# Dealing the last nine projection pieces anew over the attention heads of a hybrid encoder step

## The reference

```python
proj = h @ w_in                    # fq, fk, fv | rq, rk, rv, rg (3072 columns and 8 forget logits)
o_fox = softmax(q k^T / 8 + cq - ck, causal) @ v       # 8 heads of 64
y_ret = retention(rq, rk, rv)                           # 4 heads of 128
o_ret = silu(rg) * ret_head_norm(y_ret, gn_gain)
x = x + concat(o_fox, o_ret) @ w_out
```

## Time and profile before

| | us |
|---|---|
| median of three runs | 1013.97 |
| lowest, highest | 1012.26, 1021.46 |
| the profiled execution | 1019.17 |
| its span | 1017.4 |
| PE busy | 886.0 |
| DVE busy | 326.9 |
| ACT busy | 209.2 |
| mean granted clock of PE | 0.944 |

### The profile page before, as it was taken

The page is one execution under the profiler, slowest core; times in us unless marked ns, Lnnn a source line. Parts: engine busy times, 40 slices in busy tenths (PEclk is TensorE's granted clock), DMA queues, the critical chain, the costliest instruction groups (busy, mean ns, idle before and its releaser), DMA issues.

```text
span 1017.4 us, 14050 instructions
## 1 busy us (share of the span) xinstructions
PE 886.0 (87%) x5438; PEld 523.0 (51%) x5438; DVE 326.9 (32%) x794; ACT 209.2 (21%) x448; POOL 81.5 (8%) x93
## 2 busy tenths in 40 slices
PE   7999989899989878789768999869999978788873
PEld 5888878688733323323335555437963323233222
DVE  1514433442621101111024688872252101011103
ACT  3413223422211101011123222332121111010110
POOL 1101000000011101011010000000001111111100
PEclk9999989599899999999988999978989999999997
DMA  9713623106969999999978222304247999999965
GB/s 349 305 44 131 164 77 129 42 1 242 424 273 416 418 419 418 420 419 418 408 315 337 84 84 84 100 10 186 104 156 268 420 419 420 419 420 418 419 281 199
DMA packets 47714, 271.12 MB, mean 266 GB/s; under 512 B 10693, under 2 KB 10845, under 8 KB 18904
## 3 DMA queue, kind: packets, MB, share of 16 engines
q1 hardware_dynamic: 34416, 239.66, 58.2%
q0 software_dynamic: 11600, 24.27, 6.9%
q10 hardware_dynamic: 1632, 6.29, 1.6%
HBM read 266.54 MB, written 25.37 MB: 287 GB/s over the span
## 4 chain that ended last, share of the span: by engine, by line
PE 50%; DMA 28%; DVE 5%; issue 2%; ACT 1%; SPq 1%; ACTq 0%; POOLq 0%; DVEq 0%
DMA slot<-in_experts 23%; PE PS L985 10%; PE PS L1076 8%; PE PS L1008 7%; PE PS L826 6%; PE PS L573 3%; PE PS L803 2%; DMA XGT<-rows,IDX 2%; PE PS L966 2%; PE PS L1093 2%; DMA slot<-outs 2%; PE PS L927 1%; SPq L375 1%; PE PS L879 1%; DVE YC L1854 1%
## 5 line engine op out<-in xcount | busy, mean ns | idle before, releaser
L985 PE MATMUL PS<-slot,XG 128*64 128x512 f32 x1024 | 243.7, 621 | 64.6 <-DMA slot<-in_experts 62.5
L985 PEld LDWEIGHTS PS<-slot,XG 128*64 128x64 f32 x1024 | 78.5, 142 | 205.7 <-issue 192.9
L573 PE MATMUL PS<-slot,HT 128*128 128x256 f32 x576 | 135.0, 392 | 7.4 <-ACT HT L1157 7.4
L1738 DVE SCALAR_TENSOR_TENSOR hid_by_token<-PS,SC,SG 128x256 f32<-128x256 f32 x32 | 15.5, 484 | 391.5 <-ACT SG L1314 391.5
L573 PEld LDWEIGHTS PS<-slot,HT 128*128 128x128 f32 x576 | 111.0, 196 | 24.9 <-ACT HT L1157 7.6
L1008 PE MATMUL PS<-slot,HID 128*64 128x512 f32 x512 | 118.0, 603 | 0.9 <-ACT HID L1319 0.9
L1076 PE MATMUL PS<-HC,slot 128*128 128x384 f32 x256 | 86.0, 491 | 1.5 <-DVE HC L1814 1.5
L1314 ACT ACTIVATE SG<-PS,SC 128x256 f32<-128x256 f32 x32 | 15.2, 474 | 268.1 <-PE PS L985 268.1
L1076 PEld LDWEIGHTS PS<-HC,slot 128*128 128x128 f32 x256 | 47.6, 190 | 40.0 <-issue 9.5
L1328 ACT ACTIVATE Y<-PS,SC 128x1024 f32<-128x1024 f32 x32 | 35.6, 1114 | 152.4 <-PE PS L1008 152.4
L1008 PEld LDWEIGHTS PS<-slot,HID 128*64 128x64 f32 x512 | 35.0, 139 | 58.6 <-issue 57.2
(11 more groups left out here) (291 smaller groups left out, 821.0 us busy)
## 6 DMA issues: line engine op xcount, KB each, us to landing
slot<-in_experts SPq DMA_DIRECT2D x192, 1024.0 KB, 21.3
slot<-in_w_pw SPq DMA_DIRECT2D x12, 1024.0 KB, 8.3
slot<-in_w_in SPq DMA_DIRECT2D x11, 1024.0 KB, 10.8
slot<-outs ACTq DMA_DIRECT2D x6, 1024.0 KB, 7.0
slot<-in_w_out SPq DMA_DIRECT2D x4, 1024.0 KB, 5.2
rows<-X POOLq DMA_DIRECT2D x6, 512.0 KB, 8.5
KTC<-in_k_past POOLq DMA_DIRECT2D x1, 2048.0 KB, 13.4
slot<-in_v_past SPq DMA_DIRECT2D x2, 1024.0 KB, 8.3
```

Source lines behind the costliest of these rows:

```text
L573: last = mm(PS[:, in_bank(n), 0:UCOL], HT[:, k, P * t:P * (t + 1)], w[:, k, :], start=k == 0, stop=k == KD - 1)
L985: last = mm(PS[CAP * e:CAP * (e + 1), 2 + p % 2, :], XG[:, p % 2, k, CAP * e:CAP * (e + 1)], w[:, 2 * FE * (k % 4):2 * FE * (k % 4 + 1)], ...
```

## The change

The last nine pieces run in another order, given by a table `PIECES`: after (8,1) come (9,0), (9,1), then the two gate units (10 and 11, all tiles), and last (8,2) and (9,2), the sample tiles' values. PE and ACT place them anew: one between the K heads' transposes and the first scores, one in step 0 ahead of the transposes of the probabilities, none at the end of step 0, then one in steps 1 and 2, two in step 3, one in each of steps 4, 5 and 6. The silu of the gate moves from step 5 to step 4. The factor GN is multiplied into the retention rows after the first tile of the Q heads, long before the loop; in the loop one multiplication is left, in step 6. The retention transposes move to step 7 (tile 0) and step 8 (tiles 1 and 2); the retention projection stays from step 9 on. The waits follow: slots are free by `LAST_PIECE`, so the loads of all four `w_out` units wait for pieces 35 and 36; the sample values' store and the one behind it wait for piece 36.

```diff
+PIECES = [(pos, t) for pos in range(8) for t in range(NT)] + [(8, 0), (8, 1), (9, 0), (9, 1)] + [
+    (pos, t) for pos in (10, 11) for t in range(NT)] + [(8, 2), (9, 2)]
+LAST_PIECE = [PIECES.index((pos, 2)) + 1 for pos in range(N_IN)]
+LATE = (0, 1, 1, 2, 1, 1, 1)
...
-                    sp.wait_ge(S("proj_done"), NT * (i - LO + 1))
+                    sp.wait_ge(S("proj_done"), LAST_PIECE[i - LO])
...
-            pool.wait_ge(S("pj_ready"), 30)
+            pool.wait_ge(S("pj_ready"), 28)
             store(o["fox_v_prompt"][0].rearrange(tiles, p=P), PJ[:, 0:2, VO:RQO], "mix_stored")
+            pool.wait_ge(S("pj_ready"), 36)
             store(o["fox_v_sample"][0].rearrange(flat), PJ[:, 2, VO:RQO], "mix_stored")
...
-                    pe.wait_ge(S("pj_ready"), (26, 29, 30, 30)[i // 4])
+                    pe.wait_ge(S("pj_ready"), (26, 28, 35, 36)[i // 4])
...
+            dense_in(1)
             pe.wait_ge(S("kt_act"), NT)
...
+                if i == 0:
+                    dense_in(1)
                 if i < ITEMS:
                     probs_transposed(i)
                 if i >= 1:
                     weighted_values(i - 1)
-                if i < 6:
-                    dense_in(2 if i < 3 else 1)
+                if i < len(LATE):
+                    dense_in(LATE[i])
+                elif i == 7:
+                    ret_mixed_transposes(0)
                 elif i == 8:
-                    ret_mixed_transposes(0)
                     ret_mixed_transposes(1)
+                    ret_mixed_transposes(2)
                 elif i == 9:
-                    ret_mixed_transposes(2)
                     ret_projected(0)
...
-                    if n == 30:
+                    if n == 28:
                         act.wait_ge(S("k_ready"), NT)
...
+            evacuate(1)
+
             def exps(i):
...
-                if i < 6:
-                    evacuate(2 if i < 3 else 1)
-                if i == 5:
+                if i == 0:
+                    evacuate(1)
+                if i < len(LATE):
+                    evacuate(LATE[i])
+                if i == 4:
                     q.settle()
                     q.do(A(PJ[:, :, RGO:MIX], PJ[:, :, RGO:MIX], ACT.Silu), S("rg_silu"))
                     preload(ACT.Exp)
-                if i in (8, 9):
-                    for t in (range(2) if i == 8 else (2,)):
+                if i in (7, 8):
+                    for t in ((0,) if i == 7 else (1, 2)):
...
+                if t == 0:
+                    dve.wait_ge(S("gn_in"), 16)
+                    tt(PJ[:, :, RQO:RVO], PJ[:, :, RQO:RVO], bc(GN[:, :], 1, NT), ALU.mult)
...
                 if i == 6:
                     dve.wait_ge(S("rg_silu"), 1)
-                    dve.wait_ge(S("gn_in"), 16)
-                    tt(PJ[:, :, RGO:MIX], PJ[:, :, RGO:MIX], bc(GN[:, :], 1, NT), ALU.mult)
-                elif i == 7:
                     tt(PJ[:, :, RGO:MIX], PJ[:, :, RGO:MIX], PJ[:, :, RQO:RVO], ALU.mult, S("mixr_ready"))
```

More of the change, by code:

```diff
@@ L552, in full @@
                 pe.wait_ge(S(f"full{i % LO}"), 16 * (before + i // LO + 1 - first))
-            pieces = iter(range(NT * N_IN))
+            pieces = iter(enumerate(PIECES))
             def in_bank(n):
@@ L560, in dense_in @@
             def dense_in(m):
-                for n in itertools.islice(pieces, m):
-                    pos, t = divmod(n, NT)
+                for n, (pos, t) in itertools.islice(pieces, m):
                     w = dense(pos)
```

## The result

The changed kernel takes 1002.53 us in the median of five runs (1000.49 to 1006.78), the kernel before 1013.97 (1012.26 to 1021.46): a ratio of 0.9874 with a 95% interval of 0.9838 to 0.9911. That is faster by 1.3% (the interval leaves 0.9 to 1.6%), by 11.4 us between the medians and by 13.2 us between the means of the five runs each (1003.10 and 1016.33). The forecast was 996, in a range of 990 to 1004. The profiled execution took 1006.78 us and is the slowest of the five.

What follows compares the result with a forecast made beforehand. PE sets the pace through attention, losing time to waits and a fallen clock. Moving the first retention projection's end from 204.13 to 186.25 saves 17.9 us: 1013.97 - 17.9 = 996.1, forecast 996, range 990 to 1004.

Steps and rivals of the forecast that it cites:

- Start of the loop: Attention loop's start: pieces replace PE waits of 0.90 and 1.96 us; item 0's transposes end at 139.9.
- Steps 1 to 6: Attention loop: five steps of 5.11 us and one of 8.62, together 34.2, so step 6 ends at 174.1.
- Silu: Steps 5 and 6: 5.76 us of PE work against 5.9 us of ACT's block, leaving 0.1 to 0.5 us wait.
- The 2.66 us of the Trainium skill: ACT's table switches: by the page two would be 2.7 us longer, a sum of 998.8 instead of 996.1.
- Steps 7 to 9: Up to the retention projection: 6.9 to 7.0 us of small work plus 1.5 of waits; projection starts at 182.6.
- Loads: Four `w_out` loads leave at about 169.0 and 174.1, hidden by 3 us or more; cost 0.
- The low clock rival: Steps 7 to 9: the clock falls all the same, price 5.8 us, a time of 1002; chance 0.22.
- what the prediction drew from the Trainium skill: Steps 7 to 9: a transpose does not count as busy PE; by that rule the low clock rival is the outcome.
- the sum's base, 204.13: End of the first retention projection in the kernel before, 197.67 + 6.46, from which the forecast 186.25 was subtracted.
- the 17.9 us: Gain at the first retention projection's end: waits gone 8.45, half clock gone 10.9, less new waits 1.5.
- the likeliest case: Whole kernel: the forecast without a rival gives 996, spread 990 to 1001; chance 0.68.

Runs made afterwards that it cites:

- the first repeat of before: The kernel before, unchanged, profiled a second time: span 1015.3 us, loop 68.4 us.
- kernels with the whole or nearly the whole change: Changed kernel (two profiles) and its variants with last piece in step 5, GN in the loop, silu in step 5: spans 1005.0, 998.6, 1000.2, 1003.3, 1002.5 us.
- the run with the filler: The kernel before plus five matmuls of constants in step 7's silu wait, ahead of the transposes of the probabilities: 1012.52 us, ratio 0.9969.

## Why the prediction was right, and where it was off

*Start of the loop.* The transposes of item 0 were to end at 139.9; they begin at 139.69 in the new profile. The added multiplication on DVE cost nothing: the last K transposes start at 130.56 with it and at 130.58 in the run that has it back in the loop.

*Steps 1 to 6.* End at 174.1 by the sum; the scores of item 8 begin at 174.67, 0.6 later. The profile reached the stage 0.2 later, and the silu's wait is 0.53 us; the prediction put it at 0.1 to 0.5 but left it out of its sum.

*Silu.* The cover held. The switch of a table took 1.28 us and the silu followed at once, 1.30 us from one to the other as in the earlier trace rows. The 2.66 us of the Trainium skill, "ScalarE: Activation LUTs", section "What ACT_TABLE_LOAD costs", does not show up in this trace: no drain is to be seen between load and use.

*Steps 7 to 9.* 8.5 us by the sum, 182.84 - 174.67 = 8.2 measured. Two misses cancel in it: the waits are 0.48 and 0.18 us, 0.7 instead of 1.5, and PE's own work is 7.5 us instead of 6.9 to 7.0.

*Loads.* The four `w_out` loads were issued at 169.2, 174.8, 175.1 and 175.6 us and landed 4.7, 5.3, 10.1 and 11.9 us later. PE waited for none: the projection was released by ACT's copy. But the slack was smaller than the "3 us or more" of the prediction. The second load landed at 180.1, 2.7 us ahead of the first projection at 182.84; the last landed at 187.5, 0.8 ahead of the second one at 188.35. Row of the changed kernel's page:

```profile
slot<-in_w_out SPq DMA_DIRECT2D x4, 1024.0 KB, 7.7
```

*The low clock rival* had 0.22 and did not come. PE was busy with transposes and small matmuls alone from 174.7 to 182.8 and the clock stayed at 1.00, in both profiles of the changed kernel. In the first repeat of before the clock even rose from 0.50 near 190.5 after nothing but such work. So what the prediction drew from the Trainium skill, "TensorE: Matmul & The Clock Gate", section "Part 4: PE-mode transpose", did not come about. The page speaks of transposes alone, and of the 7.5 us in which PE is busy here they are only some 3; the rest is scores and weighted values. Whether transposes by themselves would have held the clock, no run here shows.

*The term that was mis-sized* is the sum's base, 204.13. I took it from one profile, of an execution of 1019.17 us, and subtracted the 17.9 us from a median of 1013.97. Two things were wrong in that. The loop of before takes 73.8 us in such an execution, but 68.2 to 73.8 over four, 71.0 in the mean; against 56.0 that is a gain of 15.0 us, not 17.9. I had written "over half of the gain is the clock's" and yet treated the clock's share as fixed. And the rest behind the loop varies on its own from 811.8 to 818.4 us; the first profile of the changed kernel drew the longest rest of all. 15.0 us lies close to the 13.2 between the means of the five runs each. The missing 1.8 is within that spread: the rest averages 813.6 in four profiles of before and 815.2 in the five of kernels with the whole or nearly the whole change. Whether a part of this 1.6 is systematic stays open. The way from the experts' first matmul to the convolution hints that some of it is: 266.2 to 267.6 us in the four profiles of before, 267.3 to 271.0 in those five.

The range held since its upper end came from the rival of the low clock, a rival that did not occur; for the true reason of the shortfall, the spread of the base, it would have been too narrow above (1001 for the likeliest case). The mechanism was right; that the measured 1002.53 lies in the range was luck.

## What to carry to other kernels

Where a stretch of a profile owes its length to a fallen clock, its length is a draw: profile the unchanged kernel two or three times before a gain is read off it, and subtract from the median what lies between the means. Here independent matmul groups were worth most in the places where the engines hand over to each other, ahead of the first result of a chain and behind a table load, since there one piece removes both the wait and the low clock after it. Which step the slow instruction stands in matters less than whether a piece follows it.

## What the runs showed of the hardware

The same wait of 1.96 us at the same place let the clock fall in five of six executions and not in the sixth, and the two pieces behind it took 9.50, 9.23, 8.04, 8.01, 7.90 and 6.91 us along the chain. In the kernel before, the spell behind the silu lasted until 203 in two executions and until about 190 in two others. All executions of the kernel before on these chips, 1009.95 to 1021.46 us, span 1.1%; in the profiles, 5.6 us of that is the loop alone. In the run with the last piece in step 5 the clock stood a wait of 1.55 us; in the run with the filler it was down in the stretch behind 190 to 192, in which PE was busy for 0.25 us. Ahead of the experts, behind a wait of 1.03 us, it fell in twelve of all fourteen profiles and stayed at 1.00 in two, the fastest profile of either kernel. I read no rule off these: the falls and rises of one and the same code differ between executions.
